# A whole block of modulation weights moved from the first join into the GLA scan

## The chip, the cores and the metric

The kernel runs on one core of a Trainium2 chip as one program. The metric is device microseconds (us) of one execution. Of the kernel before, three timed runs gave 3802.30, 3793.72 and 3806.67 us, with a median of 3802.3 us. A change of 0.3% is 11.4 us.

The engines are named as the profile names them: PE is the matrix engine (PEld its weight load), DVE the vector engine, ACT the scalar engine, POOL the general engine, and SP the engine that issues most DMAs. Each of SP and ACT has a DMA queue of its own.

## The reference

The program computes a hybrid layer (two scans, a mixture of experts) and a second block behind it. What matters here is the modulation of the first layer: six vectors of 1024 numbers come from one small matrix product with a large weight `ada_w` (1024 x 6144), and they are used at different places.

```python
mod_x = (jax.nn.silu(c) @ ada_w + ada_b)[:, None, :]
sh1x, sc1x, g1x, sh2x, sc2x, g2x = jnp.split(mod_x, N_MOD, axis=-1)
zx = modulate(rmsnorm(x, norm1_g), sh1x, sc1x) @ w_in
...
gla_hc, gla_hx = bidir(gla_chunked, gla_c, gla_x, gla_init)
ml_hc, ml_hx = bidir(mlstm_chunked, ml_c, ml_x, ml_init)
x = x + g1x * mixer_output(gla_hx, ml_hx, gg_x, mo_x, gla_norm_g, ml_norm_g, w_out, x.dtype)
x = x + g2x * hier_moe(modulate(rmsnorm(x, norm2_g), sh2x, sc2x), rg_w, rg_b, re_w, re_b, e_w_in, e_w_out)
```

The GLA scan keeps, for each head, a state S that is multiplied by a decay and updated with each chunk: S_t = diag(a_t) S_{t-1} + k_t^T v_t, o_t = q_t S_t. It runs over the sequence in both directions.

## The kernel before

The program is a row of stages, each ending with a barrier of all engines. Around the change they are: the value projection, the GLA scan, the mLSTM scan, the first join (it normalises and gates the outputs of both scans), and the product with `w_out`.

**Modulation.** The 6144 columns of `ada_w` are handled in three parts of 2048 (class `Modulation`, parts 0, 1 and 2). A part has eight chunks of 128 rows; a chunk is one DMA of 1 MB (`load`, line 189), which goes to one of a ring of tiles (four for parts 1 and 2) and is multiplied by four matmuls of 512 columns (`product`, line 200). After the last chunk DVE adds the bias in four instructions on one row each (`biased`, line 211), PE turns the result with four transposes (`turned`, line 216), and DVE copies 16 columns out and, for part 2, adds one to eight of them (`columns`, lines 225 and 228). Part 0 is done at the program's start. Part 1 is done beside the GLA scan, part 2 beside the first join, which calls `stage_join` with `part=2`. Part 2 is first needed after the join.

**The GLA scan** (`stage_gla`) has 20 units: 10 chunks of 128 tokens in each of the two directions, taken in turn. Units 0 to 3 are context and only update the states; units 4 to 19 also give an output. This text calls "iteration k" what an engine does for unit k in its loop. Each engine runs its own loop, and semaphores tie them:

- SP loads the inputs of unit k into one of four buffers: three DMAs for a context unit (decay, keys, values), five (with queries and transposed keys) for the others, 768 KB together. It first waits until unit k-4 is finished: its state update, and for output units its output matmuls. Then come the pieces of the modulation: the bias after unit 1, and one chunk of `ada_w` after each of the units 2, 4, ... 16. All of it goes through SP's one queue.
- PE in iteration k: the decay matmuls of unit k+2 (lines 1318 and 1319; they wait for that unit's loads), the scores of unit k+1 (line 1328; they wait for its queries), the state update of unit k (line 1344), its outputs (lines 1353 and 1354), and in the odd iterations 3 to 17 one modulation chunk (line 200). After the loop come the transposes.
- ACT in iteration k: scaled queries of unit k (line 1382), the three exponentials of unit k+2 (lines 1372 to 1374), and for units 4 to 11 the copy of the output (line 1388). It issues no DMA.
- DVE in iteration k: queries of unit k+1 (line 1420), state (line 1446), mask of unit k+1 (line 1427), for units 12 to 19 the addition into the output (line 1434), one iteration late. The bias addition of part 1 stands in iteration 18, its columns after the loop.
- POOL scales the keys.

So the loads of a unit m are issued when PE ends iteration m-4, and PE wants them at the start of iteration m-2: one iteration lies between.

**The first join** (`stage_join`) works in two rounds of four tiles: ACT squares (line 1720), PE averages (line 1740), ACT takes logarithm and exponential (lines 1725 and 1729), DVE multiplies with the gate and into the result (lines 1706 and 1708). Beside it SP issues the bias and the eight chunks of part 2, PE does four products after each round's averages, and after the second round DVE adds the bias, PE turns, DVE copies the columns.

Of the kernel before, what the change touches and what calls it, by code (L numbers as in the profile page):

```python
# [24 lines left out]
P = 128  # L25
D = 1024
KT = D // P
# [141 lines left out]
class Modulation:  # L169


    def __init__(self, K, st, g, NR):
        self.K, self.g, self.NR, self.NW = K, g, NR, 512
        self.R = 2 if g == 0 else 1
        name = f"ada{g}"
        self.w = [K.sb(f"{name}_w{i}", [P, 4, self.NW], stack=st) for i in range(NR)]
        self.bias, self.out = K.sb(f"{name}_bias", [P, self.NW], stack=st), K.sb(f"{name}_out", [P, self.NW], stack=st)
        self.pm = K.ps(f"{name}_sum", [P, self.NW], st)
        self.s_w = [K.sem(f"{name}_w{i}") for i in range(NR)]
        self.s_bias, self.s_mm, self.s_ev, self.s_t, self.s_col = (K.sem(f"{name}_{x}") for x in ("bias", "mm", "biased", "turned", "cols"))  # L180

# [3 lines left out]
    def load(self, eng, k):  # L185
        if k >= self.NR:
            eng.wait_ge(self.s_mm, k - self.NR + 1)
        src = self.K.A["ada_w"][0, k * P:(k + 1) * P, self.g * 2048:(self.g + 1) * 2048]
        eng.dma_start(self.w[k % self.NR][:], src.rearrange("p (j n) -> p j n", j=4)).then_inc(self.s_w[k % self.NR], 16)

    def load_bias(self, eng):
        for j in range(4):
            for r in range(self.R):
                c = self.g * 2048 + j * self.NW
                eng.dma_start(self.bias[32 * j + r:32 * j + r + 1, :], self.K.A["ada_b"][:, c:c + self.NW]).then_inc(self.s_bias, 16)

    def product(self, pe, k):
        pe.wait_ge(self.s_w[k % self.NR], 16 * (k // self.NR + 1))
        for j in range(4):
            mm = pe.matmul(self.pm[self.at(j), :], self.K.csil[:, k, 0:self.R], self.w[k % self.NR][:, j, :], start=k == 0, stop=k == KT - 1)  # L200
        mm.then_inc(self.s_mm, 1)
# [1027 lines left out]
def stage_gla(K):  # L1229
# [17 lines left out]
    with K.stage() as st:  # L1247
# [11 lines left out]
        po = [K.ps(f"gla_out{d}", [P, 4, P], st) for d in D2]  # L1259
        psu = K.ps("gla_update", [P, 2, P], st)  # L1260
        ada = Modulation(K, st, 1, 4)
        s_in = [K.sem(f"gla_in{b}") for b in range(NB)]
        s_init, s_ecol, s_dec, s_exp, s_qa, s_kake, s_qs, s_att, s_m, s_o, s_su, s_S, s_first, s_second = (K.sem(f"gla_{x}") for x in (
            "init", "ecol", "decay", "exp", "qa", "ka_ke", "qs", "att", "masked", "o", "su", "S", "o_copied", "o_added"))
# [5 lines left out]
        with nc.Block() as block:  # L1270
            @block.sync
            def _(sp):
                for k in range(NU):
                    b, at = k % NB, scan(k) * P
                    if k >= NB:
                        sp.wait_ge(s_su, k - NB + 1)
                        sp.wait_ge(s_kake, nkake(k - NB))
                        if isx(k - NB):
                            sp.wait_ge(s_qa, 2 * nx(k - NB))
                            sp.wait_ge(s_o, nx(k - NB))  # L1280
                    c, d = scan(k) % NCH, units[k][1]
                    sp.dma_start(lb[b][:], log_decay[c * P:(c + 1) * P, d * 256:(d + 1) * 256]).then_inc(s_in[b], 16)
                    sp.dma_start(kt[b][:], kT[at:at + P, :]).then_inc(s_in[b], 16)
                    sp.dma_start(v[b][:], vT[at:at + P, 0:512].rearrange("t (h p) -> t h p", p=P)).then_inc(s_in[b], 16)
                    if isx(k):
                        sp.dma_start(q[b][:], gq[:, at - NCTX:at - NCTX + P].rearrange("(a p) t -> p a t", p=P)).then_inc(s_in[b], 16)
                        sp.dma_start(k_[b][:], gk[:, at:at + P].rearrange("(a p) t -> p a t", p=P)).then_inc(s_in[b], 16)
                    if k == 1:
                        ada.load_bias(sp)
                    if k >= 2 and k % 2 == 0 and k // 2 - 1 < KT:  # L1290
                        ada.load(sp, k // 2 - 1)

            @block.gpsimd
            def _(pool):
# [15 lines left out]
            def _(pe):  # L1310
# [21 lines left out]
                for k, (j, d) in enumerate(units):  # L1332
# [13 lines left out]
                    if isx(k):  # L1346
# [6 lines left out]
                            pe.matmul(po[u][:, h, :], v[b][:, h, :], att[u][:, h, :], start=True, stop=False)  # L1353
                            mm = pe.matmul(po[u][:, h, :], S[d][j % 2][:, h // 2, :], qs[u][:, h, :], start=False, stop=True)
                        mm.then_inc(s_o, 1)
                    if k >= 3 and k % 2 and k // 2 - 1 < KT:
                        ada.product(pe, k // 2 - 1)
                ada.turned(pe)

            @block.scalar  # L1360
            def _(act):
# [31 lines left out]
                for k in range(NU):  # L1393
                    if isx(k):
                        states(k)
                    if k + 2 < NU:
                        exps(k + 2)
                    if isx(k) and first(k):
                        copied(k)

            @block.vector
            def _(dve):
# [32 lines left out]
                for k, (j, d) in enumerate(units):  # L1435
# [16 lines left out]
                        added(k - 1)  # L1452
                    if k == 2:
                        ada.clear(dve)
                    if k == NU - 2:
                        ada.biased(dve)
                if not first(NU - 1):
                    added(NU - 1)
                ada.columns(dve)


def stage_mlstm(K):
# [286 lines left out]
def mixer_one(K):  # L1749
# [29 lines left out]
    stage_mlstm(K)  # L1779
    with ExitStack() as st:  # L1780
        mixF = K.mixF
        stage_join(K, "join1", [(None, "gla_norm_g", ggF, 0), (None, "ml_norm_g", moF, 4)], mixF, part=2)
        parts = tuple(K.sb(f"mixF_{x}", [P, KT, T], stack=st) for x in ("hi", "lo"))
        stage_gemm_f(K, "wout1", [(A["w_out"][0], D, None, None, 1.0, False)], parts, T, whole=[mixF[:, k, :] for k in range(KT)], residual=K.hF, gcol=mc[:, 16:24])
    K.mixstack.close()
# [1747 lines left out]
```

## Time and profile before

| | us |
|---|---|
| median of three timed runs | 3802.3 |
| lowest and highest | 3793.72, 3806.67 |
| profiled execution, device time | 3808.09 |
| its span | 3806.2 |
| GLA scan, from the first DMA issue (505.53) to that of the next stage (625.75) | 120.2 |
| first join, from its first DMA issue (742.37) to that of the next stage (790.88) | 48.5 |

The profiled execution is one run, 5.8 us above the median; 1.9 us of its time lie outside the span. Every time below is from its trace, in microseconds from the span's start. In a timeline row the first number is the start, the second the time from start to end of the merged instructions (count at the end); the brackets hold the engine's idle time before the row and what ended it. A PE row of 128x512 f32 that is counted x8 is four matmuls of the program: each runs as two.

### The profile page before, as it was taken

The numbers are of one execution on the slowest core, as the hardware profiler recorded it, in microseconds if no ns is written. First come the engines' busy times: TensorE is split into PE (matmuls) and PEld (weight loads), VectorE is DVE, ScalarE is ACT, GpSimd is POOL, SyncE is SP. The second block draws the span as 40 slices with busy tenths as digits, with TensorE's granted clock in tenths as the row PEclk, the third lists the DMA queues.
The fourth block names the chain that finished last, engine by engine and source line by source line (L and its number), as shares of the span: only waits on it lengthen the run. The fifth ranks groups of instructions, "written<-read, shape, count | busy, mean of one in ns | idle before, by whom it ended". The sixth has DMA issues, their size and how long they took to land. (4 is left out here: it accounts for less than half of the span.)

```text
span 3806.2 us, 50262 instructions
## 1 busy us (share of the span) xinstructions
PE 3252.2 (85%) x18142; PEld 2588.0 (68%) x18142; DVE 2128.4 (56%) x3058; ACT 1250.1 (33%) x1906; POOL 228.0 (6%) x334
## 2 busy tenths in 40 slices
PE   6998977777899999966998697485779989998977
PEld 4776766554688888844886695274648877887765
DVE  5221844453899999963111673654457755775543
ACT  4211222513688888843000424313031100110111
POOL 2000012300111111100000000000000000000000
PEclk8998988988899999978999899798889999999988
DMA  6233667833686699931322201101113322332121
GB/s 234 91 106 118 192 209 204 244 110 123 258 318 256 254 385 362 361 132 55 99 91 75 72 26 42 58 3 46 55 47 93 93 83 88 94 94 77 61 66 44
DMA packets 383534, 515.73 MB, mean 135 GB/s; under 512 B 48313, under 2 KB 287616, under 8 KB 379952
## 3 DMA queue, kind: packets, MB, share of 16 engines
q1 hardware_dynamic: 343696, 443.36, 34.6%
q10 hardware_dynamic: 25600, 46.41, 3.5%
q0 software_dynamic: 14112, 24.23, 1.8%
q8 instruction: 86, 1.41, 0.2%
q14 instruction: 40, 0.33, 0.0%
HBM read 455.79 MB, written 81.17 MB: 141 GB/s over the span
## 5 line engine op out<-in xcount | busy, mean ns | idle before, releaser
L2172 DVE TENSOR_TENSOR exp_w_lo<-exp_w_raw,exp_w_hi 128x1024 fp32r<-128x1024 f32 x378 | 435.6, 1219 | 4.4
L2120 ACT ACTIVATE exp_w_hi<-exp_w_raw 128x1024 fp32r<-128x1024 f32 x378 | 371.0, 1055 | 7.7 <-PE exp_up_psum L405 7.7
L403 PE MATMUL in_ps_psum<-hN_hi,in_wh 128*128 128x512 f32 x720 | 286.8, 398 | 32.4 <-DVE in_wl L397 32.3
L403 PE MATMUL up_ps_psum<-hN_hi,up_wh 128*128 128x512 f32 x704 | 281.0, 399 | 30.5 <-DVE up_wl L397 30.5
L404 PE MATMUL in_ps_psum<-hN_lo,in_wh 128*128 128x512 f32 x720 | 285.1, 396 | 0.0
L405 PE MATMUL in_ps_psum<-hN_hi,in_wl 128*128 128x512 f32 x720 | 284.6, 395 | 0.0
L404 PE MATMUL up_ps_psum<-hN_lo,up_wh 128*128 128x512 f32 x704 | 280.6, 399 | 0.0
L405 PE MATMUL up_ps_psum<-hN_hi,up_wl 128*128 128x512 f32 x704 | 280.4, 398 | 0.0
L395 DVE CAST in_wh<-in_w 128x1024 fp32r<-128x1024 f32 x45 | 31.2, 694 | 399.1 <-PE in_ps_psum L405 393.8
L403 PE MATMUL exp_up_psum<-exp_w_hi,exp_x_hi 128*128 128x512 f32 x592 | 231.6, 391 | 3.9 <-DVE exp_w_lo L2172 3.9
L404 PE MATMUL exp_up_psum<-exp_w_lo,exp_x_hi 128*128 128x512 f32 x592 | 231.0, 390 | 0.0
L405 PE MATMUL exp_up_psum<-exp_w_hi,exp_x_lo 128*128 128x512 f32 x592 | 231.0, 390 | 0.0
L3249 ACT ACTIVATE up_z<-up_ps_psum 128x512 f32<-128x512 f32 x88 | 52.9, 601 | 424.1 <-PE up_ps_psum L405 424.1
L403 PEld LDWEIGHTS in_ps_psum<-hN_hi,in_wh 128*128 128x128 f32 x720 | 137.1, 190 | 70.5 <-DVE in_wl L397 33.5
L403 PEld LDWEIGHTS up_ps_psum<-hN_hi,up_wh 128*128 128x128 f32 x704 | 133.6, 190 | 64.3 <-DVE up_wl L397 31.8
L403 PE MATMUL down_ps_psum<-down_ah,down_wh 128*128 128x512 f32 x352 | 138.8, 394 | 23.5 <-DVE down_al L397 23.5
L405 PEld LDWEIGHTS in_ps_psum<-hN_hi,in_wl 128*128 128x128 f32 x720 | 137.0, 190 | 30.9
L404 PEld LDWEIGHTS in_ps_psum<-hN_lo,in_wh 128*128 128x128 f32 x720 | 137.0, 190 | 29.8
L405 PEld LDWEIGHTS up_ps_psum<-hN_hi,up_wl 128*128 128x128 f32 x704 | 133.5, 190 | 32.7
L404 PEld LDWEIGHTS up_ps_psum<-hN_lo,up_wh 128*128 128x128 f32 x704 | 133.6, 190 | 32.5
L3267 DVE SCALAR_TENSOR_TENSOR up_conv<-up_z,cols,up_conv 128x512 f32<-128x512 f32 x176 | 132.3, 752 | 24.2 <-DVE up_conv L3265 6.1
L404 PE MATMUL down_ps_psum<-down_al,down_wh 128*128 128x512 f32 x352 | 138.4, 393 | 0.0
(651 smaller groups left out, 7034.4 us busy)
## 6 DMA issues: line engine op xcount, KB each, us to landing
exp_w_raw<-in_expert_w_in SPq DMA_DIRECT2D x256, 512.0 KB, 6.0
up_w<-in_ffn_up SPq DMA_DIRECT2D x88, 512.0 KB
exp_w_raw<-in_expert_w_out SPq DMA_DIRECT2D x64, 512.0 KB, 6.8
hF<-in_expert_w_out SPq DMA_DIRECT2D x64, 512.0 KB, 4.9
ada_w<-in_ada_w SPq DMA_DIRECT2D x24, 1024.0 KB, 9.0
in_w<-in_w_in SPq DMA_DIRECT2D x44, 512.0 KB, 4.2
down_w<-in_ffn_down SPq DMA_DIRECT2D x44, 512.0 KB
wout_w<-in_w_out SPq DMA_DIRECT2D x16, 512.0 KB, 3.7
```

What stands on the lines that cost most here:

```text
L395: dve.tensor_copy(hi.bitcast(F32R), x).then_inc(s_hi, 1)
L403: pe.matmul(out, r(w[0]), r(x[0]), start=start, stop=False)
L404: pe.matmul(out, r(w[0]), r(x[1]), start=False, stop=False)
L405: return pe.matmul(out, r(w[1]), r(x[0]), start=False, stop=stop)
L2120: act.activation(wh[:, c, :].bitcast(F32R), raw[c], ACT.Copy).then_inc(s_wh, 1)
L2172: dve.tensor_tensor(wl[:, c, :].bitcast(F32R), raw[c], wh[:, c, :], ALU.subtract).then_inc(s_wl[c], 1)
L3249: act.activation(z[u][g][:, 2:], pm[u][g][:], ACT.Copy).then_inc(s_z[u], 1)
L3267: step(dve.scalar_tensor_tensor(o, z[u][g][:, n:n + BANK], taps(j, g, n), o, ALU.mult, ALU.add))
```

## The change

- The scan carries both parts. A second `Modulation` object for part 2 reuses the tiles, the bias row, the output row and the PSUM bank of part 1 (`older=ada`), and so waits on part 1's semaphores where it reuses them.
- The loads leave SP's queue. ACT issues one chunk per iteration: part 1 in iterations 0 to 7, part 2 in iterations 9 to 12 and 14 to 17; the biases in iterations 1 and 13. In ACT's loop they stand last in the iteration.
- PE does a product in each of the iterations 2 to 9 (part 1) and 12 to 19 (part 2), the transposes of part 1 in iteration 11, those of part 2 after the loop.
- DVE adds the bias of part 1 in iteration 10 and copies its columns in iteration 12; bias and columns of part 2 come after the loop.
- The first join has no modulation part: its eight chunks, products, bias addition, transposes and columns are gone from there.

```diff
@@ class Modulation
     def load(self, eng, k):
         if k >= self.NR:
             eng.wait_ge(self.s_mm, k - self.NR + 1)
+        elif self.older is not None:
+            eng.wait_ge(self.older.s_mm, KT - self.NR + k + 1)
...
     def load_bias(self, eng):
+        if self.older is not None:
+            eng.wait_ge(self.older.s_ev, 5)
...
     def product(self, pe, k):
         pe.wait_ge(self.s_w[k % self.NR], 16 * (k // self.NR + 1))
+        if k == 0 and self.older is not None:
+            pe.wait_ge(self.older.s_col, self.older.R)
@@ stage_gla, SP
-                    if k == 1:
-                        ada.load_bias(sp)
-                    if k >= 2 and k % 2 == 0 and k // 2 - 1 < KT:
-                        ada.load(sp, k // 2 - 1)
@@ PE
-                    if k >= 3 and k % 2 and k // 2 - 1 < KT:
-                        ada.product(pe, k // 2 - 1)
-                ada.turned(pe)
+                    if 2 <= k < 2 + KT:
+                        ada.product(pe, k - 2)
+                    if k == 11:
+                        ada.turned(pe)
+                    if 12 <= k < 12 + KT:
+                        ada2.product(pe, k - 12)
+                ada2.turned(pe)
@@ ACT
+                    if k == 1:
+                        ada.load_bias(act)
+                    if k < KT:
+                        ada.load(act, k)
+                    if k == 13:
+                        ada2.load_bias(act)
+                    if 9 <= k <= 12:
+                        ada2.load(act, k - 9)
+                    if 14 <= k <= 17:
+                        ada2.load(act, k - 10)
@@ DVE
-                    if k == NU - 2:
+                    if k == 10:
                         ada.biased(dve)
+                    if k == 12:
+                        ada.columns(dve)
+                        ada2.clear(dve)
...
-                ada.columns(dve)
+                ada2.biased(dve)
+                ada2.columns(dve)
@@ mixer_one
-        stage_join(K, "join1", [...], mixF, part=2)
+        stage_join(K, "join1", [...], mixF)
```

How the instructions stand on ACT in the scan, iteration 4 and the start of iteration 5, in the kernel before (`gla_qs` scaled queries, `gla_e_...` the three exponentials of unit 6, `mixF` the copy of the output):

```order
L1382 ACTIVATE gla_qs<-gla_qa,gla_decay_cols 128x256 x2
L1372 ACTIVATE gla_e_mid<-gla_decay_psum 128x256
L1373 ACTIVATE gla_e_inv<-gla_decay_psum 128x256
L1374 ACTIVATE gla_e_end<-gla_decay_psum 128x256
L1388 ACTIVATE mixF<-gla_out_psum 128x4x128
L1382 ACTIVATE gla_qs<-gla_qa,gla_decay_cols 128x256 x2
```

The same place after the change:

```order
L1392 ACTIVATE gla_qs<-gla_qa,gla_decay_cols 128x256 x2
L1382 ACTIVATE gla_e_mid<-gla_decay_psum 128x256
L1383 ACTIVATE gla_e_inv<-gla_decay_psum 128x256
L1384 ACTIVATE gla_e_end<-gla_decay_psum 128x256
L1398 ACTIVATE mixF<-gla_out_psum 128x4x128
L194 DMA ada_w<-in_ada_w 128x2048
L1392 ACTIVATE gla_qs<-gla_qa,gla_decay_cols 128x256 x2
```

A chunk is issued right after the copy of the unit's output and ahead of the next unit's scaled queries, where nothing stood before. On SP's queue only the loads of the units are left.

On DVE, iterations 10 and 11 of the scan, in the kernel before (`gla_qa` queries, `gla_S` the state, `gla_att` the mask):

```order
L1446 SCALAR_TENSOR_TENSOR gla_S_0<-gla_S_1,gla_decay_cols,gla_update_psum 128x128 x2
L1427 COPY_PREDICATED gla_att<-gla_mask,gla_att_psum 128x512
L1420 TENSOR_TENSOR gla_qa<-gla_q,gla_e_mid 64x2x128 x2
L1446 SCALAR_TENSOR_TENSOR gla_S_0<-gla_S_1,gla_decay_cols,gla_update_psum 128x128 x2
L1427 COPY_PREDICATED gla_att<-gla_mask,gla_att_psum 128x512
```

The same place after the change:

```order
L1466 SCALAR_TENSOR_TENSOR gla_S_0<-gla_S_1,gla_decay_cols,gla_update_psum 128x128 x2
L1447 COPY_PREDICATED gla_att<-gla_mask,gla_att_psum 128x512
L220 TENSOR_TENSOR ada_out<-ada_sum_psum,ada_bias 1x512 x4
L1440 TENSOR_TENSOR gla_qa<-gla_q,gla_e_mid 64x2x128 x2
L1466 SCALAR_TENSOR_TENSOR gla_S_0<-gla_S_1,gla_decay_cols,gla_update_psum 128x128 x2
```

The four bias additions of part 1 now stand ahead of the queries of unit 12. Before, they stood in iteration 18, where no queries followed.

## Rows read from the trace of the kernel before

**Rows 1.** The page: the span

```profile
span 3806.2 us, 50262 instructions
```

**Rows 2.** Windows: PE, PEld, DVE, ACT, POOL busy (count), PEclk, DMA share, GB/s

```profile
505.00:625.00 120.00, 96.26 (x716) 75.50 (x716) 47.26 (x108) 35.36 (x94) 27.04 (x38) 0.85 0.61 193
```

**Rows 3.** Timeline, end of the first join: start us, busy us, engine, line

```profile
775.41 1.28 DVE L1706 SCALAR_TENSOR_TENSOR join_rstd<-join_rstd,cols,join_gate 128x1024 f32<-128x1024 f32 x1 [7.76 <-ACT join_rstd L1729]
...
784.09 1.22 DVE L1708 TENSOR_TENSOR mixF<-mixF,join_rstd 128x1024 f32<-128x1024 f32 x1
785.24 2.83 DVE L211 TENSOR_TENSOR ada_out<-ada_sum_psum,ada_bias 1x512 f32<-1x512 f32 x4
...
788.12 1.12 PE L216 MATMUL ada_sum_psum<-const,ada_out 128*128 128x128 f32 x4 [5.50 <-DVE ada_out L211]
...
789.49 0.17 DVE L228 TENSOR_SCALAR modcols<-modcols 128x8 f32<-128x8 f32 x1
790.88 6.32 SPq L534 DMA_DIRECT2D wout_w<-in_w_out  x3
```

**Rows 4.** Timeline of PE in the first join

```profile
744.78 9.41 PE L1740 MATMUL join_ps_psum<-join_sq,const 128*128 128x512 f32 x16 [3.96 <-ACT join_sq L1720]
...
758.81 1.04 PE L200 MATMUL ada_sum_psum<-ada_w,cond_silu 128*1 128x512 f32 x8 [1.45 <-DMA ada_w<-in_ada_w]
...
762.97 8.83 PE L1740 MATMUL join_ps_psum<-join_sq,const 128*128 128x512 f32 x16 [0.64 <-ACT join_sq L1720]
```

**Rows 5.** Timeline of PE in the scan, iterations 5 to 19

```profile
539.96 0.61 PE L1318 MATMUL gla_decay_psum<-const,gla_log_decay 128*128 128x128 f32 x4
...
552.64 0.71 PE L1318 MATMUL gla_decay_psum<-const,gla_log_decay 128*128 128x128 f32 x4 [2.66 <-DMA gla_k<-gkF]
...
558.15 0.71 PE L1318 MATMUL gla_decay_psum<-const,gla_log_decay 128*128 128x128 f32 x4
...
559.13 1.05 PE L1328 MATMUL gla_att_psum<-gla_qa,gla_ka 128*128 128x128 f32 x8
...
562.59 0.64 PE L1318 MATMUL gla_decay_psum<-const,gla_log_decay 128*128 128x128 f32 x4
...
576.24 1.23 PE L1318 MATMUL gla_decay_psum<-const,gla_log_decay 128*128 128x128 f32 x4 [3.61 <-DMA gla_k<-gkF]
...
584.49 0.71 PE L1318 MATMUL gla_decay_psum<-const,gla_log_decay 128*128 128x128 f32 x4
...
610.89 0.71 PE L1318 MATMUL gla_decay_psum<-const,gla_log_decay 128*128 128x128 f32 x4 [0.73 <-DMA gla_k<-gkF]
...
616.39 1.16 PE L1328 MATMUL gla_att_psum<-gla_qa,gla_ka 128*128 128x128 f32 x8
...
622.30 0.39 PE L1354 MATMUL gla_out_psum<-gla_qs,gla_S 128*128 128x128 f32 x2
```

**Rows 6.** Timeline of SP's DMA issues in the scan

```profile
508.27 1.17 SPq L195 DMA_DIRECT2D ada_bias<-in_ada_b  x4
...
542.53 0.47 SPq L189 DMA_DIRECT2D ada_w<-in_ada_w  x1
544.55 0.33 SPq L1282 DMA_DIRECT2D gla_log_decay<-gla_la  x1
...
604.74 0.33 SPq L1282 DMA_DIRECT2D gla_log_decay<-gla_la  x1
```

**Rows 7.** Timeline of ACT, end of iteration 7

```profile
557.29 0.60 ACT L1388 ACTIVATE mixF<-gla_out_psum 128x512 f32<-128x512 f32 x1 [2.52 <-PE gla_out_psum L1354]
```

**Rows 8.** Timeline of DVE: queries in iteration 8, and the scan's end

```profile
561.97 1.14 DVE L1420 TENSOR_TENSOR gla_qa<-gla_q,gla_e_mid 64x256 f32<-64x256 f32 x2
...
624.51 0.17 DVE L225 COPY modcols<-ada_sum_psum 128x16 f32<-128x16 f32 x1
```

**Rows 9.** Timeline of PE at the scan's start

```profile
519.73 1.22 PE L1319 MATMUL gla_decay_psum<-gla_log_decay,const 128*128 128x256 f32 x2 [2.78 <-DMA gla_v<-vT]
...
529.17 1.22 PE L1318 MATMUL gla_decay_psum<-const,gla_log_decay 128*128 128x128 f32 x4 [3.57 <-DMA gla_k<-gkF]
```

More of the change, by code:

```diff
@@ L169, with __init__ @@
 class Modulation:
-    def __init__(self, K, st, g, NR):
-        self.K, self.g, self.NR, self.NW = K, g, NR, 512
+    def __init__(self, K, st, g, NR, older=None):
+        self.K, self.g, self.NR, self.NW, self.older = K, g, NR, 512, older
         self.R = 2 if g == 0 else 1
         name = f"ada{g}"
-        self.w = [K.sb(f"{name}_w{i}", [P, 4, self.NW], stack=st) for i in range(NR)]
-        self.bias, self.out = K.sb(f"{name}_bias", [P, self.NW], stack=st), K.sb(f"{name}_out", [P, self.NW], stack=st)
-        self.pm = K.ps(f"{name}_sum", [P, self.NW], st)
+        if older is None:
+            self.w = [K.sb(f"{name}_w{i}", [P, 4, self.NW], stack=st) for i in range(NR)]
+            self.bias, self.out = K.sb(f"{name}_bias", [P, self.NW], stack=st), K.sb(f"{name}_out", [P, self.NW], stack=st)
+            self.pm = K.ps(f"{name}_sum", [P, self.NW], st)
+        else:
+            self.w, self.bias, self.out, self.pm = older.w, older.bias, older.out, older.pm
         self.s_w = [K.sem(f"{name}_w{i}") for i in range(NR)]
@@ L1261, in stage_gla @@
         ada = Modulation(K, st, 1, 4)
+        ada2 = Modulation(K, st, 2, 4, older=ada)
         s_in = [K.sem(f"gla_in{b}") for b in range(NB)]
@@ L1781, in mixer_one @@
         mixF = K.mixF
-        stage_join(K, "join1", [(None, "gla_norm_g", ggF, 0), (None, "ml_norm_g", moF, 4)], mixF, part=2)
+        stage_join(K, "join1", [(None, "gla_norm_g", ggF, 0), (None, "ml_norm_g", moF, 4)], mixF)
         parts = tuple(K.sb(f"mixF_{x}", [P, KT, T], stack=st) for x in ("hi", "lo"))
```

## The prediction, made before the changed kernel had run

> **What bounds the kernel now.** I first read the page for the size of the whole: 3806.2 us of span [rows 1]. The change touches two stages, so I read those in the timeline. In the first join PE and DVE are not the bound: DVE waits 7.76 us for ACT's exponential before its second round [rows 3], and the second round's averages on PE wait only for ACT's squares (0.64 us) [rows 4]. Part 2 costs the join nothing while ACT sets the pace; what it costs is its end. DVE's last result is there at 784.09 + 1.22 = 785.31, and behind it come bias, transposes and columns until 789.49 + 0.17 = 789.66 [rows 3].
>
> In the scan, PE is busy 96.26 of 120 us and the DMA engines 61% [rows 2]. PE's timeline shows two kinds of iterations. Iteration 8, without a product, takes 562.59 - 558.15 = 4.44 us; iteration 7, with one, takes 558.15 - 552.64 = 5.51 [rows 5]. Between them PE waits for loads: 2.66 us ahead of iteration 7, 3.61 ahead of iteration 11, 0.73 ahead of iteration 17 [rows 5]. After the 3.61 PE comes back at half clock (the decay matmuls take 1.23 instead of 0.71 us), and that iteration takes 584.49 - 576.24 = 8.25 us, 2.74 more than 5.51 [rows 5]. Why it waits is in SP's issues. A unit's loads are issued when PE ends iteration m-4 and wanted one iteration later. With the queue free (unit 19) they need 610.89 - 604.74 = 6.15 us; unit 9, whose loads stand behind a chunk issued 2 us earlier (542.53), needs 552.64 - 544.55 = 8.09 [rows 5, 6]. So the latency L of a unit's loads and PE's work W in an iteration share the time: start(k) = start(k-2) + W + L where L is longer than W. The period is (W + L)/2, and an iteration waits (L - W)/2.
>
> **The change, term by term**, against the profiled execution's 3808.09 us.
>
> 1. Join. The end goes: 789.66 - 785.31 = 4.35 us less. Eight loads go from SP's queue; the gates were not waited for, so that is worth 0. Without products between the rounds PE rests some 9 us before its second round. In the first round, after a rest, the same sixteen matmuls took 9.41 us, in the second 8.83 [rows 4]; I add the difference, 0.6. Bounds: 0 (ACT hides it) and 1.2 (both slower). The product with `w_out` begins after a long rest in either kernel: 0. Sum: -3.8 us.
>
> 2. Scan's start. The bias (1.17 us of SP) no longer stands between units 1 and 2 [rows 6], and the first chunk comes on ACT behind the exponentials of unit 2, so the loads of units 2 and 3 are alone. The waits for unit 3 (2.78 us) and unit 5 (3.57 us) [rows 9] were behind chunks. The first shrinks to about nothing; then chunks 1 to 3 are issued one per iteration beside units 5 to 7, and product 0 and the one in iteration 4 are new (1.2 us each at half clock). I hand 5 us back of the 6.4 and take -1.5. Bounds: -5 (no collision) and +2.
>
> 3. Iterations 5 to 17. Before: 616.39 - 539.96 = 76.4 us [rows 5]. After: 13 x 4.44 = 57.7, eleven products of 1.04 (the row of a product [rows 4]) = 11.4, transposes in iteration 11 about 0.6: 69.7 without a wait. That is 6.7 less than before, although four products are added, because 11.6 us of that stretch were waits and half clock. Which waits come? A chunk moves in 1.45 + 1.04 = 2.49 us when chunks follow each other [rows 4]. The DMA engines were busy 0.61 x 120 = 73 us; without eight chunks that is 53 us for 20 units, 2.7 each [rows 2, 4]. Now every iteration carries 2.7 + 2.5 = 5.2 us of transfers, just under W = 5.5: throughput holds, latency doesn't. For units 4 to 11 ACT ends the output copy 0.6 us after PE's last output (557.29 + 0.60, with PE's outputs until 557.2 [rows 7]) and issues the chunk, exactly when SP issues unit k+4's five loads. If these wait for the whole chunk, L = 6.15 - 1.0 (the lower end of what the loads need when nothing is beside them: iterations 8 and 9 didn't wait [rows 5]) + 2.5 = 7.65. Eight iterations (5 to 9, 11 to 13) then wait (7.65 - 5.5)/2 = 1.1 each: 8.8. In iterations 12 to 17 the chunk is issued behind the exponentials, some 2 us into the iteration, when most of the unit's data is in; four iterations wait (6.15 - 5.5)/2 = 0.3: 1.3. Bounds of the collision for one iteration: 0 (nothing waits) and (9.0 - 5.5)/2 = 1.8, with L as of the unit ahead of the half-clock iteration (its wait of 3.61 [rows 5] less the 0.7 of unit 19 and 6.15 give 9.0).
>
> DVE's bias addition in iteration 10 puts its 2.83 us [rows 3] ahead of the queries of unit 12. In iteration 8 the queries start 561.97 - 558.15 = 3.8 us into the iteration and take 1.1; PE wants them 559.13 - 558.15 = 1.0 us into the next one, at 5.4 [rows 5, 8]. Now they are ready at 7.8: PE stalls 2.4 us, unless it waits for loads at that moment anyway. I take 1.0 (bounds 0 and 2.4). ACT's own issues (0.47 us each on SP [rows 6]) stand before scaled queries that PE wants 2.7 us later: 0. The chunk waits on ACT are for products two or more iterations old: 0. Sum: 69.7 + 8.8 + 1.3 + 1.0 = 80.8, so +4.4 us.
>
> 4. Iteration 18 has a product and had none: +1.0 us.
>
> 5. Scan's end. Before, the last output matmul ended at 622.30 + 0.39 = 622.69 and DVE at 624.51 + 0.17 = 624.68 [rows 5, 8]: 2.0 us. Now a product of 1.04 comes first, and then the same tail that left the join, 4.35 us: with a step of 0.1 it is 5.5. +3.5 us. Nothing covers it, since the last addition of DVE is done by then.
>
> Sum: -3.8 - 1.5 + 4.4 + 1.0 + 3.5 = +3.6 us. The profiled execution was 3808.1, so 3811.7; against the median of the runs, 3802.3, that is 3806. The point of the change, the tail of the join, comes back almost whole at the end of the scan.
>
> What two queues are worth is where a page bears. By the rows, unit 9 lost 1.9 us behind a chunk in its own queue, and another queue could spare it that: no collision, rival A below. The Trainium skill, DMA: Bandwidth & Descriptors, section "Issuing engines are not separate DMA queues", says that DMAs from either engine run on the same sixteen DMA engines and interleave, and that a second issuer saves only issue time. By that rule the unit's loads still share with the chunk, and the sum stays as above. No row of this case shows two queues loaded together.
>
> **The rivals.**
>
> A. The collisions cost little: the unit's small loads slip between the chunk's. For it: iteration 9 shows no wait though a chunk had been issued one iteration before its unit [rows 5]. Against it: 8.09 against 6.15 us. Price: the 8.8 goes, the stall on queries shows more (+1), the start gains 2 more: 3.6 - 8.8 + 1 - 2 = -6 us, 3796.
>
> B. Slower: loads and chunk together reach PE's clock. The point from which it decides is the gap after which PE came back at half clock, 3.61 us; 2.66 didn't do it [rows 5]. With L = 9.0 in all eight iterations, waits gather in the first ones, and the chunk beside each load keeps it so. Price: 8 x (1.8 - 1.1) = 5.6, and half clock in three iterations, 3 x 2.74 = 8.2: 3.6 + 13.8 = +17 us, 3820. Against it: waits come back every iteration and are short, not one long one.
>
> C. ACT is held at its issues (queue full), and the exponentials and the scaled queries are late. SP's issues mostly take 0.3 to 0.5 us [rows 6]; to delay PE's outputs an issue would have to take over 1.1 us (2.7 less 0.6, 0.5 and 0.5 for the first half of the scaled queries). Price: 8 x 0.5 = 4 more, 3810.
>
> **Numbers.** Chances: forecast 0.48, A 0.24, B 0.16, C 0.12. What this measurement can tell from no change is 0.3%, 11.4 us: below 3790.9 is faster, above 3813.7 slower. The forecast and A lie inside; faster needs A with the best start (-5) and no stall, 0.06. Slower is most of B, a little of C: 0.15. The range joins A's and B's sides: from -8 (no collision at all, start at -4) to +13 (all collisions at 1.8, stall 2.4, start +1), 3794 to 3816.
>
> **What would show it.** In the changed profile: the join ends about 4 us earlier against its start; between PE's last output and the next stage's first DMA lie some 6.5 us instead of 3; PE's iterations 5 to 9 show waits on `gla_k` of about 1 us each instead of two of 2.7 and 3.6; there is a stall on `gla_qa` in iteration 11; DMA share of the scan rises from 0.61 to about 0.75. The forecast is wrong if the scan from its first load to the next stage takes under 122 us or over 134 instead of some 128 (120.2 plus 7.4), or if PE's clock there falls well below 0.85 [rows 2].

## The result: slower by half a per cent

Twenty runs of each kernel gave a median of 3831.65 us for the changed kernel (3818.33 to 3839.61) and 3808.74 us for the one before (3793.72 to 3833.46, the first three runs among them). The ratio of the runs is 1.0051, with a 95% interval of 1.0039 to 1.0064. By it the change costs some 19 us (15 to 24 by the interval); the forecast was +3.6, and the time lies above the upper end of the range, 3816. The median of before moved from 3802.3 (three runs) to 3808.7 (twenty), so ratios are compared below, not single medians.

The profiled execution took 3827.64 us, 19.55 more than that of before. Its span:

```profile
span 3825.8 us, 50262 instructions
```

By the stages' first DMA issues, the join takes 43.45 us instead of 48.51, and the scan 144.02 instead of 120.22. The mLSTM scan between them takes 117.26 instead of 116.62, and the rest is scatter of a few us in stages that nobody touched. So one number has to be explained: the scan's +23.8, where +7.4 was forecast. The prediction named a scan over 134 us as a sign that it is wrong, and the scan is 144. The window over the scan of the changed kernel (columns as in [rows 2]):

```profile
508.27:652.29 144.02, 107.00 (x784) 77.95 (x784) 50.43 (x115) 35.72 (x94) 27.02 (x38) 0.85 0.66 219
```

PE has 68 matmuls more, and its mean clock is 0.85 in either kernel. The share of DMA hardly rose, from 0.61 to 0.66, where the forecast said about 0.75. A stage that moves a third more bytes at nearly the same share has become longer by waiting, not by transferring. Cut at PE's iterations, the scan is, in us:

| stretch | before | after | forecast |
|---|---|---|---|
| first load to start of iteration 5 | 34.43 | 37.16 | 32.9 |
| iterations 5 to 11 | 44.53 | 41.95 | 44.5 |
| iterations 12 to 17 | 31.90 | 51.21 | 36.4 |
| iteration 18 to the next stage | 9.36 | 13.70 | 13.9 |

(Term 3 is split by its own terms: 7 x 4.44 + 5 x 1.04 + 0.6 + 6 x 1.1 + 1.0 = 44.5, and 6 x 4.44 + 6 x 1.04 + 2 x 1.1 + 1.3 = 36.4.) The third line holds nearly everything. PE's timeline of the changed kernel shows the waits from iteration 2 on (line 1324 is what line 1318 was; 1.49 us ahead of iteration 4 and 0.19 ahead of 12 are left out):

```profile
528.26 1.23 PE L1324 MATMUL gla_decay_psum<-const,gla_log_decay 128*128 128x128 f32 x4 [7.05 <-DMA gla_k<-gkF]
...
545.43 0.71 PE L1324 MATMUL gla_decay_psum<-const,gla_log_decay 128*128 128x128 f32 x4 [1.49 <-DMA gla_k<-gkF]
...
557.54 0.71 PE L1324 MATMUL gla_decay_psum<-const,gla_log_decay 128*128 128x128 f32 x4 [1.03 <-DMA gla_k<-gkF]
...
564.41 0.71 PE L1324 MATMUL gla_decay_psum<-const,gla_log_decay 128*128 128x128 f32 x4 [1.30 <-DMA gla_k<-gkF]
...
581.82 0.71 PE L1324 MATMUL gla_decay_psum<-const,gla_log_decay 128*128 128x128 f32 x4 [1.79 <-DMA gla_k<-gkF]
...
598.01 1.22 PE L1324 MATMUL gla_decay_psum<-const,gla_log_decay 128*128 128x128 f32 x4 [5.05 <-DMA gla_k<-gkF]
...
614.25 0.71 PE L1324 MATMUL gla_decay_psum<-const,gla_log_decay 128*128 128x128 f32 x4 [3.41 <-DMA gla_k<-gkF]
615.23 1.76 PE L1334 MATMUL gla_att_psum<-gla_qa,gla_ka 128*128 128x128 f32 x8
...
630.68 1.23 PE L1324 MATMUL gla_decay_psum<-const,gla_log_decay 128*128 128x128 f32 x4 [3.80 <-DMA gla_k<-gkF]
```

These are iterations 2, 5, 7, 8, 11, 13, 15 and 17. Those from 5 to 11 are the 1 to 1.8 us that the forecast gave them. Those at 13, 15 and 17 are 3.4 to 5.05 us, and after each PE works at half clock for a while: the decay matmuls take 1.22 instead of 0.71 us, or the scores 1.76 instead of 1.05. These three iterations take 7.25, 7.06 and 7.91 us instead of 5.5. So the 51.2 us are six times 5.5 (33.0), the three waits (12.3) and half clock (some 5.7). What PE waited for at 630.68 is in the DMA queues. The issues of the changed kernel around it (start, us of issue, queue):

```profile
606.26 0.47 SPq L1297 DMA_DIRECT2D gla_k<-gkF  x1
606.45 0.36 ACTq L194 DMA_DIRECT2D ada_w<-in_ada_w  x1
...
622.30 0.47 SPq L1297 DMA_DIRECT2D gla_k<-gkF  x1
622.50 0.33 ACTq L194 DMA_DIRECT2D ada_w<-in_ada_w  x1
```

and the times from issue to landing for the loads of unit 19, which were issued from 620.50 to 622.30 (last number, us; the five loads of a unit count up one semaphore, and the view ascribes its counts to them in the order of issue):

```profile
gla_v<-vT SPq DMA_DIRECT2D x1, 256.0 KB, 2.7
gla_log_decay<-gla_la SPq DMA_DIRECT2D x1, 128.0 KB, 2.0
gla_kT<-gkT SPq DMA_DIRECT2D x1, 128.0 KB, 2.6
gla_q<-gqF SPq DMA_DIRECT2D x1, 128.0 KB, 3.5
gla_k<-gkF SPq DMA_DIRECT2D x1, 128.0 KB, 8.3
```

The first four land about as in the kernel before (medians there 2.8, 2.2, 2.3 and 2.8 us). The fifth, issued 0.2 us before the chunk, takes 8.3 us. It is 128 KB; the median for it in the kernel before is 3.3:

```profile
gla_k<-gkF SPq DMA_DIRECT2D x16, 128.0 KB, 3.3
```

Unit 17 is alike, only that its queries are late too (2.1, 2.2, 2.7, 5.5 and 7.9 us in the order of issue). The whole scan of the changed kernel has a median of 5.7:

```profile
gla_k<-gkF SPq DMA_DIRECT2D x16, 128.0 KB, 5.7
```

The two ends went nearly as forecast. The last product starts behind the last output, and bias, transposes and columns follow (timeline of the changed kernel, the scan's end):

```profile
645.47 0.39 PE L1360 MATMUL gla_out_psum<-gla_qs,gla_S 128*128 128x128 f32 x2
645.79 1.04 PE L209 MATMUL ada_sum_psum<-ada_w,cond_silu 128*1 128x512 f32 x8
...
646.95 2.84 DVE L220 TENSOR_TENSOR ada_out<-ada_sum_psum,ada_bias 1x512 f32<-1x512 f32 x4 [0.37 <-PE ada_sum_psum L209]
649.85 1.12 PE L225 MATMUL ada_sum_psum<-const,ada_out 128*128 128x128 f32 x4 [3.02 <-DVE ada_out L220]
...
651.21 0.17 DVE L237 TENSOR_SCALAR modcols<-modcols 128x8 f32<-128x8 f32 x1
652.29 0.33 SPq L1537 DMA_DIRECT2D ml_kT<-mkT  x1
```

From the last output matmul's end (645.86) to the last column (651.38) are 5.5 us, as worked out. And the join ends with DVE's last result at 811.85, with nothing of the modulation behind it; the second row is the first DMA of the next stage:

```profile
810.63 1.22 DVE L1732 TENSOR_TENSOR mixF<-mixF,join_rstd 128x1024 f32<-128x1024 f32 x1
813.00 6.34 SPq L543 DMA_DIRECT2D wout_w<-in_w_out  x3
```

### The profile page after: what moved, and what is told of

Its sections match the earlier page's. It is cut to its first block and busy times, and to the rows that moved or that the text cites. A ratio compares the mean times of both kernels' runs of the same rounds, so it can differ in the third digit from the quotient of the medians.

```text
span 3825.8 us, 50262 instructions
## 1 busy us (share of the span) xinstructions
PE 3247.4 (85%) x18142; PEld 2586.1 (68%) x18142; DVE 2128.3 (56%) x3058; ACT 1250.4 (33%) x1906; POOL 227.8 (6%) x334
## 5 line engine op out<-in xcount | busy, mean ns | idle before, releaser
L414 PEld LDWEIGHTS in_ps_psum<-hN_hi,in_wl 128*128 128x128 f32 x720 | 136.9, 190 | 30.9
L413 PEld LDWEIGHTS in_ps_psum<-hN_lo,in_wh 128*128 128x128 f32 x720 | 136.9, 190 | 29.9
L412 PE MATMUL wout_ps_psum<-mixF_hi,wout_wh 128*128 128x512 f32 x256 | 102.3, 400 | 52.4 <-DVE mixF_lo L406 52.0
```

The source lines that it names most:

```text
L412: pe.matmul(out, r(w[0]), r(x[0]), start=start, stop=False)
L413: pe.matmul(out, r(w[0]), r(x[1]), start=False, stop=False)
L414: return pe.matmul(out, r(w[1]), r(x[0]), start=False, stop=stop)
```

## The experiments

Ratios are to the kernel before on the same chip, from runs taken in turn, with 95% intervals. "Scan" is the time from its first DMA issue to that of the next stage in the profiled execution, and "late stretch" iterations 12 to 17 of it. Each trace is one execution. Up to iteration 11 the changed kernel, e2, e10 and e11 have the same instructions; the stretch before iteration 5 took 37.2, 35.5, 40.7 and 36.7 us in them, and iterations 5 to 11 took 42.0, 42.3, 44.4 and 42.1. So a difference of a few us between two traces can be scatter.

| kernel | ratio | interval | scan | late stretch |
|---|---|---|---|---|
| before | 1 | | 120.2 | 31.9 |
| changed kernel | 1.0051 | 1.0039 to 1.0064 | 144.0 | 51.2 |
| e1 all chunks on SP's queue | 1.0006 | 0.9986 to 1.0026 | 125.0 | 35.1 |
| e2 late chunks later on ACT | 1.0018 | 1.0005 to 1.0031 | 131.7 | 40.6 |
| e4 12 of 16 chunks of 8 KB | 1.0171 | 1.0146 to 1.0196 | 125.5 | 34.2 |
| e5 six buffers | 0.9974 | 0.9959 to 0.9990 | 122.2 | 32.9 |
| e6 before, six buffers | 0.9952 | 0.9933 to 0.9970 | 106.1 | 29.8 |
| e7 before, its chunks on ACT | 0.9991 | 0.9976 to 1.0007 | 123.6 | 32.8 |
| e8 e5, bias behind the queries | 0.9971 | 0.9957 to 0.9986 | 117.6 | 32.9 |
| e9 the three together | 0.9963 | 0.9948 to 0.9977 | 113.9 | 32.9 |
| e10 late chunks on SP, same moment | 1.0012 | 0.9996 to 1.0028 | 134.4 | 36.0 |
| e11 the pair of chunks parted | 1.0043 | 1.0023 to 1.0063 | 136.9 | 44.3 |
| e12 e6, chunks begin later | 0.9952 | 0.9934 to 0.9971 | 99.4 | 29.8 |

**e1, queue.** All sixteen chunks go back to SP's queue, each behind a unit's loads; products and tails stay.

```
 SP, unit k:   + if 4 <= k < 12:  ada.load(sp, k - 4)
               + if 12 <= k < 20: ada2.load(sp, k - 12)
 ACT:          - if k < KT: ada.load(act, k)   ... and the rest of its chunk loads
```

> The changed kernel with all sixteen chunks back in SP's queue, one behind the loads of each of the units 4 to 19; the products stay where the change put them. Theory P (place): a chunk hurts where it runs beside a unit's last small loads on another queue; in one queue behind them it is done before the next unit's loads start. Then PE has no wait over 2 us in iterations 5 to 19, these take 75 to 80 us up to the start of 18 (changed kernel: 93.2), the scan 122 to 128 us (144.0), and the kernel is level with the one before (ratio 0.998 to 1.001). Theory D (density): one megabyte per iteration is too much wherever it is issued; then the scan stays above 138 us and the ratio at 1.004 to 1.006.

The scan falls from 144.0 to 125.0 us, with the same work and the same bytes. No wait from iteration 12 on is over 0.9 us, where it was 3.4 to 5.05:

```profile
597.08 0.71 PE L1328 MATMUL gla_decay_psum<-const,gla_log_decay 128*128 128x128 f32 x4 [0.47 <-DMA gla_k<-gkF]
603.54 0.71 PE L1328 MATMUL gla_decay_psum<-const,gla_log_decay 128*128 128x128 f32 x4 [0.89 <-DMA gla_k<-gkF]
609.60 0.71 PE L1328 MATMUL gla_decay_psum<-const,gla_log_decay 128*128 128x128 f32 x4 [0.48 <-DMA gla_k<-gkF]
```

The window over its scan moves more per us at a higher share, and PE has a better clock:

```profile
514.94:639.94 125.00, 103.38 (x784) 75.52 (x784) 50.41 (x115) 35.62 (x94) 26.98 (x38) 0.90 0.75 253
```

So neither the number of products nor the bytes make the 20 us. But e1 changes queue, moment and spacing at once.

**e2, moment.** The chunks of the second half are issued at the end of an iteration, behind its outputs.

```
 ACT, end of iteration k:
               + if 12 <= k <= 17: act.wait_ge(s_o, nx(k))
```

> The changed kernel, but ACT waits in iterations 12 to 17 for the unit's outputs before it issues the chunk, so that the second half issues at the same point as the first. Theory P: the waits before iterations 13, 15 and 17 (5.05, 3.41, 3.80 us) fall to about 1 to 1.5 each and the half clock goes; iterations 12 to 17 take 38 to 41 us instead of 51.2, the ratio is 1.001 to 1.003. Theory D: 48 to 52 us as now, ratio 1.004 to 1.006.

The late stretch falls from 51.2 to 40.6 us, and the join and the rest are untouched. The moment at which a chunk is issued gives back 10.6 of the 16 us that e1 gives back. Waits of 2.16 us are left ahead of iterations 13 and 16, longer than the 1 to 1.5 that I expected, and half clock isn't gone either: the decay matmuls after them take 0.71 us, but the scores 1.77 and 1.60, and each of the two iterations takes 7.06 us instead of 5.5 (columns as in [rows 2]; the granted clock is the 0.76):

```profile
592.98:600.04 7.06, 7.06 (x46) 5.47 (x46) 2.57 (x6) 1.79 (x5) 1.42 (x2) 0.76 0.51 183
```

**e10, queue at nearly the same moment.** The late chunks are issued when the changed kernel issues them (SP waits for ACT's exponentials), but from SP's queue and behind the unit's loads.

```
 SP, unit k:   + if k in (15, 17, 18, 19):
               +     sp.wait_ge(s_exp, k)
               +     ada2.load(sp, k - 12 if k == 15 else k - 13)
               + ...                              # the last chunk behind the loop
 ACT:          - if 9 <= k <= 12:  ada2.load(act, k - 9)
               + if 9 <= k <= 11:  ada2.load(act, k - 9)
               - if 14 <= k <= 17: ada2.load(act, k - 10)
```

> The changed kernel; the five chunks that ACT issues in iterations 12 and 14 to 17 are issued by SP at the same moment (after the same exponentials), so that they stand behind the unit's last loads in one queue instead of beside them in another. Theory O (order of queues): a small load that is out first but on the other queue is held until most of the chunk is through (gla_k took 7.9 and 8.3 us from issue to landing in the changed kernel, 3.3 at the median before); in one queue it lands in 3 to 5 us. Then the waits before iterations 15 and 17 (3.41, 3.80 us) go, iterations 12 to 17 take 35 to 40 us instead of 51.2, ratio 1.000 to 1.003. Theory M (moment): one megabyte at that moment fills the DMA engines whoever issues it; then gla_k lands in 7 us or more and the stretch stays at 48 to 52, ratio 1.004 to 1.006.

The late stretch is 36.0 us. The issues of this kernel, the second of each pair the chunk:

```profile
608.54 0.47 SPq L1297 DMA_DIRECT2D gla_k<-gkF  x1
609.70 0.34 SPq L194 DMA_DIRECT2D ada_w<-in_ada_w  x1
```

and how long the two took (window of these issues):

```profile
ada_w<-in_ada_w SPq DMA_DIRECT2D x1, 1024.0 KB, 5.9
gla_k<-gkF SPq DMA_DIRECT2D x1, 128.0 KB, 3.1
```

The same load needs 3.1 us, and for the next two units 5.1 and 4.4, where it needed 7.9 and 8.3 with the chunk on the other queue. But the chunk comes 1.2 us behind the load here, not 0.2, so e10 changed two things: the queue, and the distance to the load. Other runs have the two apart. In e7, below, the chunk comes on ACT's queue 1.14 us behind the last load of unit 17:

```profile
601.87 0.47 SPq L1287 DMA_DIRECT2D gla_k<-gkF  x1
603.01 0.34 ACTq L189 DMA_DIRECT2D ada_w<-in_ada_w  x1
606.26 0.61 PE L1314 MATMUL gla_decay_psum<-const,gla_log_decay 128*128 128x128 f32 x4
```

The third row is PE at the start of iteration 15, which needs this load, and it did not wait: the load was in within 4.4 us. Collected from the traces, the landing of a unit's last load, by the place of the chunk behind it:

| chunk's queue | behind the last load, us | units | landing, us |
|---|---|---|---|
| ACT's | 0.0 to 0.2 | 17 and 19 of the changed kernel, 19 of e11, e5, e8 | 7.9, 8.3, 7.6, 7.0, 7.0 |
| ACT's | 1.14 | 17 of e7 | at most 4.4 |
| ACT's | 2.1 and 3.1 | 18 of e11, 18 of the changed kernel | 3.9, 3.9 |
| SP's | 0.5 | 12 to 19 of e1 | 3.8 to 5.7 |
| SP's | 1.1 to 1.8 | 17 to 19 of e10 | 3.1, 5.1, 4.4 |

So it takes both, the other queue and a chunk right behind the load. In the load's own queue half a us is enough, and on the other queue a distance of 1.1 us was, in the one case there is. Whether the late chunks could stay on ACT's queue if all of them came a us later, no run shows.

Its first stretch took 40.7 us, 3.5 more than in the changed kernel with the same instructions there, which is why its whole scan is not shorter than e2's.

**e11, the pair.** In iterations 11 and 12 the changed kernel issues two chunks 1.8 us apart (586.80 and 588.58), both beside unit 15. Here the second comes an iteration later.

```
 ACT:          - if 9 <= k <= 12: ada2.load(act, k - 9)
               + if 9 <= k <= 11 or k == 13: ada2.load(act, {9: 0, 10: 1, 11: 2, 13: 3}[k])
```

> The changed kernel with the chunk of iteration 12 issued in iteration 13. In the changed kernel the chunks of iterations 11 and 12 are 1.8 us apart, both beside the loads of unit 15, whose last load took 9.1 us. If the pair is what made the 5.05 us wait before iteration 13, that wait falls under 2 us, and one of about 3.5 us with half clock comes before iteration 14, where none was (unit 16 now has a chunk beside its last load): iterations 12 to 17 stay at 46 to 52 us, ratio 1.004 to 1.006. If the pair was the main loss, the stretch falls under 44 us.

The wait ahead of iteration 13 goes from 5.05 to 2.20 us and the late stretch from 51.2 to 44.3, between my two alternatives; the wait that I expected ahead of iteration 14 did not come. The ratio (1.0043) can't be told from that of the changed kernel. Iterations 15 and 17 still wait, 2.41 and 3.27 us: a single chunk on the other queue, 0.3 us ahead of the last load of unit 17 and together with that of unit 19, is enough. And e10 still has two chunks beside unit 15 (593.57 on ACT's queue, 596.36 on SP's), but its wait ahead of iteration 13 is 2.25 us. So what the pair cost is again a chunk close beside the last load on the other queue: the second one of the changed kernel comes 0.3 us ahead of it (588.58 and 588.88), and that load took 9.1 us.

**e4, bytes.** Twelve of the sixteen chunks bring 8 KB instead of 1 MB. The later stages take other times by that, so only its scan is read.

```
 load(k):      + if self.g and (k >= self.NR or self.older is not None):
               +     ... dma_start(self.w[k % self.NR][:, 0, 0:16], ...)   # 16 columns
```

> The changed kernel with the chunks 4 to 7 of part 1 and all of part 2 loading 16 columns (8 KB) instead of 2048: the products are the same instructions on wrong data. Both P and D: waits for loads and half clock go from the scan except at its start; iterations 5 to 17 take 70 to 76 us, the scan 118 to 124 us, ratio 0.996 to 0.999. Theory W (the products and the tail themselves are the cost): the scan stays over 135 us, ratio 1.003 or more.

The late stretch is 34.2 us and the median landing of the load 3.6 us. So it is the transfer of the chunk that holds the load, and not ACT's issue, which stays. One wait of 1.15 us is left there. The scan, 125.5 us, is above the 118 to 124 that I expected: its start is as long as in the changed kernel, because the first four chunks are whole. PE's timeline of e4 shows a stall of another kind, in iteration 11:

```profile
583.11 1.16 PE L1338 MATMUL gla_att_psum<-gla_qa,gla_ka 128*128 128x128 f32 x8 [2.12 <-DVE gla_qa L1444]
```

This is the bias addition ahead of the queries. In the changed kernel DVE did the same (579.25 + 2.83, then the queries at 582.11), but PE waited for its loads meanwhile until 581.82.

**e5 and e6, lead.** The changed kernel, and the one before, with six input buffers instead of four: loads are issued two iterations earlier.

```
 -    NB, NCX = 4, NCTX // P
 +    NB, NCX = 6, NCTX // P
```

> The changed kernel with six buffers for a unit's loads instead of four, so that they are issued two iterations earlier. If latency behind a lead of one iteration is what turns collisions into waits (P, and the recurrence of the prediction), nearly all waits after iteration 6 go: iterations 5 to 17 take 70 to 76 us, the scan 117 to 124 us, ratio 0.996 to 0.999. If the transfers' throughput is the bound (D), waits of the same sum stay and the ratio is 1.003 to 1.006.

> The kernel before the change with six buffers for a unit's loads. If its own 11.6 us of waits and half clock in iterations 5 to 17 come from the short lead too, the scan falls from 120.2 to 106 to 111 us and the ratio is 0.996 to 0.998, below the six-buffer form of the changed kernel (0.9974) by what the change still costs when no load is waited for: eight products of 1.04 us and 3.5 us of tail, less 5 us of join, 7 us. Against it: if the chunks in SP's queue held the scan by throughput, it stays at 118 or more.

In e5 no iteration after the fourth waits for a load, although the median landing is 6.3 us, longer than in the changed kernel. In e9, below, it is 7.7 us, and no iteration waits there either. The landing time costs nothing when two more units are under way. The window over the scan of e5:

```profile
505.24:627.45 122.21, 101.60 (x784) 75.22 (x784) 50.46 (x115) 35.50 (x95) 26.72 (x39) 0.90 0.77 259
```

and its row of PE's timeline in iteration 11:

```profile
575.72 2.08 PE L1334 MATMUL gla_att_psum<-gla_qa,gla_ka 128*128 128x128 f32 x8 [2.11 <-DVE gla_qa L1440]
```

The stall on the queries now costs its whole 2.11 us and half clock behind it (2.08 instead of 1.05 us): iteration 11 takes 8.69 us. And e6 has a shorter scan than e5 and a lower ratio, though the intervals overlap: with the waits gone, the eight products and the tail are dearer in the scan than in the join. The ratio of e6, 0.9952, is a little below the 0.996 to 0.998 that I expected. The window over its scan:

```profile
504.19:610.29 106.10, 92.56 (x716) 72.58 (x716) 47.26 (x108) 35.15 (x94) 27.04 (x38) 0.87 0.66 219
```

122.2 - 106.1 = 16.1 us more in the scan, against 48.4 - 43.9 = 4.5 us less in the join. About half of the 16.1 is the stall and the start of the scan: e9, below, which removes these, is 113.9 - 106.1 = 7.8 us above e6.

**e8, the bias.** e5 with DVE's bias addition moved behind the queries of iteration 11.

```
 DVE:          - if k == 10: ada.biased(dve)
               + if k == 11: ada.biased(dve)      # behind the queries
```

> The six-buffer form of the changed kernel with DVE's bias addition of part 1 moved from behind iteration 10 into iteration 11 between the queries and the wait for the state update, where DVE idles 3.2 us. It prices the stall that iteration 11 shows there (8.7 us instead of 5.1: 2.11 us on the queries and half clock after it): the scan 118.5 to 119.5 us instead of 122.2, ratio 0.996 to 0.9975. If DVE's addition isn't the cause, 122.

The scan goes from 122.2 to 117.6 us, a little under the expected 118.5 to 119.5; iteration 11 takes 4.78. The ratio (0.9971) can't be told from that of e5: 4.6 us are 0.12%, and the intervals are wider.

**e7, queue alone.** The kernel before, with its eight chunks on ACT's queue at the end of the even iterations.

```
 SP:           - if k >= 2 and k % 2 == 0 and k // 2 - 1 < KT: ada.load(sp, k // 2 - 1)
 ACT:          + if k % 2 == 0 and k // 2 < KT: ada.load(act, k // 2)
```

> The kernel before the change with nothing but the queue changed: part 1's eight chunks and the bias are issued by ACT, last in iterations 0, 2, ... 14, part 2 stays in the join. Theory P: a chunk now falls beside the loads of the unit after its iteration instead of behind them; the scan's waits stay about as large as before (scan 117 to 126 us, ratio 0.998 to 1.002), so neither queue is faster by itself. If the second queue itself were the cost (Q), the scan grows by a good part of the changed kernel's 24 us already with eight chunks: 128 or more, ratio over 1.002.

The scan takes 123.6 us, 3.4 more, with half clock behind a wait of 3.67 us and behind two of 2.11 and 2.25; the time of the kernel doesn't differ. At this spacing, a chunk in every second iteration and none within a us of a unit's last load, the queue hardly matters.

**e9 and e12, can it be had?** e9 is e8 with the chunks on SP's queue. e12 is e6 with the bias at unit 7 and the first chunks at units 5 and 6, so that the first units load alone.

```
 e12, SP:      - if k == 1: ada.load_bias(sp)
               + if k == 7: ada.load_bias(sp)
               - if k >= 2 and k % 2 == 0 and k // 2 - 1 < KT: ada.load(sp, k // 2 - 1)
               + if k == 5: ada.load(sp, 0)
               + if k >= 6 and k % 2 == 0 and k // 2 - 2 < KT: ada.load(sp, k // 2 - 2)
```

> The changed kernel with six buffers, the bias addition in DVE's gap and the chunks behind the unit loads in SP's queue (behind units 3 to 10 and 12 to 19). The start of the scan, where the loads of unit 4 were waited for 7 us beside two chunks, loses most of that: scan 112 to 118 us, ratio 0.994 to 0.997. Theory Q' (with six buffers the place no longer matters): the same as the run with the bias addition in the gap alone, 118.5 to 119.5.

> The kernel before the change with six buffers, part 1's chunks behind units 5, 6, 8, ... 18 instead of 2, 4, ... 16 and the bias behind unit 7, so that nothing stands between the first units' loads. The waits for units 3 and 5 (2.91 and 1.72 us in the six-buffer form) go: scan 101 to 104 us instead of 106.1, ratio 0.994 to 0.995, the fastest form. If the start is bound by the loads themselves, 106.

e9 is the best form of the change (scan 113.9) and still behind e6 in the scan; their ratios can't be told apart. e12 has the shortest scan, 99.4 us, where 101 to 104 was expected (its window):

```profile
511.06:610.49 99.43, 88.42 (x716) 69.70 (x716) 47.28 (x108) 35.37 (x95) 26.71 (x39) 0.94 0.70 233
```

Its 6.7 us against e6 don't show in the ratio (0.9952 for both). Either is some 0.5% faster than the kernel before and 1% faster than the changed one.

## Why the prediction was wrong, step by step

**Term 3, iterations 12 to 17: the step that failed.** The prediction put it so: the chunk is issued "some 2 us into the iteration, when most of the unit's data is in; four iterations wait (6.15 - 5.5)/2 = 0.3". The 2 us are right, counted from the first of the unit's five loads: 604.46 to 606.45. But the five issues take 1.8 us, so the chunk comes 0.2 us behind the last, and at 606.45 none of the five had landed (the first did at 604.46 + 2.1 = 606.56). I counted from the group's first load where its last one mattered. The price of an overlap was low as well: the forecast let a chunk add its 2.5 us to a unit's loads; measured, the last load takes 7.9 and 8.3 us, 4.6 and 5.0 over the 3.3 of before. The stretch had 36.4 us in the forecast, 3.5 of it waits, and took 51.2, 12.3 of it waits and some 5.7 half clock, which stood in the sum at nothing and only in rival B. The runs undo it in different ways: e2, with the moment moved, gives back 10.6 us; e10, with SP's queue and a us more distance, 15.2; e11, the pair parted alone, 6.9. Read as a division of one loss, about 7 us are the pair at iterations 11 and 12, whose second chunk the prediction didn't see beside unit 15 at all, and about 8 (44.3 - 36.0) the chunks at the last loads of units 17 and 19; with one trace each these are rough. What they have in common is a chunk on the other queue within 0.3 us of a unit's last load.

**Term 3, iterations 5 to 11: right.** 41.95 us against 44.5; the waits are 1.03 to 1.79 us, with 1.1 forecast, but ahead of four iterations instead of six. Where the chunk is issued together with the first load, as for unit 11, the five loads take 5.2 to 5.5 us each: all share with it, and none stands out (only for unit 10 the last took 6.7).

**The stall on queries: the mechanism right, its size hidden.** Bounds were 0 and 2.4. Iteration 11 waited 1.79 us for its loads already. In e1, e4 and e5 the stall is 1.60, 2.12 and 2.11 us, and e8 takes it away.

**Term 2, the start: wrong in sign.** Forecast -1.5, measured +2.7. "The loads of units 2 and 3 are alone" is true, but those of unit 4 are not: PE waited 7.05 us for it, since it was issued (519.04 to 520.83) between chunk 0 (517.99) and chunk 1 (521.60), with the bias. The bound, +2, was too narrow. In e1, whose first chunk comes at unit 4, this wait is 3.23 us.

**Term 1, the join: right, a little low.** 48.51 - 43.45 = 5.06 us less, forecast 3.8. The 0.6 us that I added for PE's rest don't show: the averages after it took 8.77 us and not 9.4, as in the second round of before [rows 4], and DVE's wait for the exponential is 7.70 us as before [rows 3]. The tail is gone as forecast. The remaining 0.6 us lie ahead of DVE's last result (42.3 us into the join instead of 42.9): the first round's averages took 8.83 us and not 9.41. Why isn't shown.

**Terms 4 and 5: right.** 4.3 us together in the last line of the first table, forecast 4.5.

**The rivals.** A fell: it has a scan of some 118 us (120.2 - 6 + 3.8), and the best run of the same work with four buffers, e1, has 125.0. B named the mechanism that made the time: loads and chunk together bring gaps of 3.41 to 5.05 us, and half clock comes behind three of them; its +17 us is near the 19. But 3.61 us is no bound: in e2 half clock came behind 2.16 us. And its place was wrong (it had the eight early iterations with the chunk beside the loads), and the forecast that long gaps would not occur because "waits come back every iteration and are short" failed in the late ones, where the unit's last load alone was held. C fell: ACT's chunk issues take 0.33 to 0.37 us, and e4, with the same issues, has no such waits.

One thing on which I leaned needs a correction. The Trainium skill, DMA: Bandwidth & Descriptors, section "Issuing engines are not separate DMA queues", has DMAs of all issuers interleave on the same engines. On throughput the runs agree: for the same bytes the engines were busy 0.66 x 144 = 95 us with two queues and 0.75 x 125 = 94 with one (e1). I took from it that the choice of queue leaves the sum as it is. For the latency of a load just issued the runs say otherwise: 3.8 to 5.7 us with the chunk 0.5 us behind it in its own queue, 7.0 to 8.3 with the chunk up to 0.2 us behind it on the other.

**What stays open.** Why the earlier load of one queue is passed by a later transfer of the other isn't shown by the views read here, which give times of whole DMAs. That a us of distance is enough on ACT's queue rests on one unit of e7, whose chunks are far apart; between 0.2 and 1.1 us no unit has a single chunk there. No run compares the two queues at one and the same distance below 1.1 us. And why PE loses its clock behind one wait of 2.2 us and not behind another isn't shown either.

## What to carry to other kernels

A large transfer on a second queue isn't hidden because the queue is free: ask which small load is still under way when it is issued, count from the issue of the last load of the group, and keep the large one behind the loads in their own queue or well clear of the last load, or give the loads more lead. With two more buffers the same landing times cost nothing: depth took 0.8% off the changed kernel and 0.5% off the one before, the best placing of the chunks with four buffers (e1) 0.45% off the changed kernel. And before work is moved out of a stage, price what it costs there: eight products that hid behind ACT in the join cost 1 us each, and a tail, in a scan that PE sets.

## What the runs showed of the hardware

- A 128 KB load issued up to 0.2 us before a 1 MB load on another queue took 7.0 to 8.3 us (five cases; median before 3.3). With the 1 MB load 0.5 us behind it in the same queue it took 3.8 to 5.7 (e1, eight units), and with the 1 MB load 1.14 us behind on the other queue at most 4.4 (e7, one unit). With the 1 MB load 2.1 to 2.5 us ahead of it on the other queue (units 8 to 11, 13 and 14 of the changed kernel) it took 4.7 to 5.3, once 6.7.
- PE came back at half clock after gaps of 5.05, 3.80 and 3.67 us; after 3.41 the first decay matmuls took 0.71 us and the scores 1.76. After one wait of 2.20 us in e11 the decay matmuls took 1.21; after 2.16 in e2 they took 0.71 and the scores 1.77 (granted clock of the iteration 0.76); after 2.41 in e11 and 2.66 in the kernel before the whole iteration ran at full clock (5.50 and 5.51 us). The gap alone doesn't decide it.
- Half clock behind a gap made an iteration of 5.5 us 1.6 to 2.4 us longer (changed kernel and e2).
